# Ring loads at once, the scale's chunk first, k tiles outermost, biases ahead of the modulation

## The chip, the cores and the metric

The kernel runs on one NeuronCore of one Trainium2 chip. The metric is device time in microseconds (us) for one launch; lower is better. Five engines with their own instruction streams work side by side: TensorE (PE, its weight loads PEld), VectorE (DVE), ScalarE (ACT), GpSimd (POOL) and SyncE (SP, which here only issues DMAs). TensorE's granted clock is either 2.4 GHz (written 1.00) or 1.2 GHz (0.50).

## The reference, cut to what matters

`x` is 256 tokens by 1024 channels, float32. Five stages follow each other, each reading the `x` that the one before left:

```
h = rmsnorm(x, g) * (1 + scale) + shift        # scale, shift, gate = chunks of silu(c) @ ada_w + ada_b
x = x + gate * (mixer(h @ in_w) @ out_w)
```

The stages are called EVEN (pooling and spatial gating), ODD (gated linear attention and stick-breaking attention), F1 (SwiGLU feed-forward), MIX (short convolution and a state-space mixer) and F2 (a second SwiGLU). Between ODD and F1 stands one more rmsnorm, at the end a last one. `x` and the conditioning vectors are small; the weights, some 210 MB of float32, are read once from HBM.

## The kernel before, in words

**Number format.** Every float32 product runs as three reduced-precision (fp32r) matmuls: a weight piece is split into a high part `WH` (a copy by ACT, function `cut`, line 1083) and a low part `WL` (weight minus `WH`, by DVE, line 1505); an activation likewise into `hh`/`hl` or `YH`/`YL`. `mm3` issues high*high, high*low, low*high into one PSUM region.

**Pieces and the ring.** A unit of weights is 1 MB; it travels as two halves of 512 KB, `[128, 1024]` each, in a ring of `RING = 10` slots in SBUF. SP issues the loads in the order of `unit_list`, each waiting until the slot's last user is done. A half of a main unit is a piece: ACT cuts piece n+3 and DVE piece n+2 while PE is at piece n; `WH` and `WL` have four buffers each, freed by `s_use` when PE has used them. Between the main units stand the `ada` units (the conditioning weights), which DVE multiplies by silu(c) and sums into `ACC` (lines 1518, 1521), half by half.

**Conditioning.** A chunk is 1024 columns of `ada_w`: chunk 0 the shift, 1 the scale, 2 the gate. Each has eight halves. For the first two chunks some halves (`ADA_PE`) are done by PE instead, straight into the PSUM tensor `pacc`; for the others `ada(key)` on PE sums `ACC` over the partitions into a bank (the "sum"), and `ada(key)` on DVE adds the bias into `MOD` (the "add", line 1531) and so frees that bank. `plan` says at which unit each step stands; those with a key "tail ..." stand at a stage's end.

**Stage start.** DVE's `modulate` (lines 1595 to 1607) makes, for each of eight k tiles of 128 channels, `SQT[k] = xT[k] * GS[k] * r` (the u tile, line 1601), ACT adds the shift and rounds it to `hh[k]`, and DVE forms `hl[k]` (line 1606). PE's `cols_T`, `cols_N` and `ffn` then take a unit half by half: half 0 uses k tiles 0 to 3, half 1 uses 4 to 7, for two output tiles m; the loop over m is outside, that over k inside. One unit is 2 x 2 x 4 x 3 = 48 matmuls.

**Stage end.** `out_rows` adds two 128-row blocks (halves h = 0, 1) into the eight tiles of `pacc`. In a stage's last such unit (eo7, oo7, f1d10, wo3, f2d10) pairs of finished tiles are signalled; DVE's `update` adds them to `xT` (line 1615), ACT squares them into `SQT` (line 1118), PE sums the squares over channels (`stats`, bank `fin`), DVE takes the reciprocal root (Newton steps, lines 1564 to 1572), PE spreads it (`spread`, bank `r`). At the end of ODD PE also spreads a second factor (`xnew`, line 967). `warm` issues matmuls with no use but to keep PE busy. The four banks `pw0` to `pw3` go round by `open_` and `back`; PE waits at `open_` until a bank's last reader is done.

**Start of the program.** SP issues nine small loads (`pack_loads(0)`: c, norm_g, ada_b, ... cond), then the ring; ACT loads the identity, `x` and the rest of the constants; POOL the other small vectors. PE turns the vectors (`vc0`) and `x` (`xt0` to `xt3`) round, DVE makes `SIL` = silu(c), and the first two chunks run. The four lines of the start on DVE that matter most:

```python
cut(1 - AHEAD_L)
ada("p4")
mod_cols(0, M0, "norm_g")
modulate(L_EVEN, M0[:, 0:8])
```

Of the kernel before, what the change touches and what calls it, by code (L numbers as in the profile page):

```python
# [54 lines left out]
ADA_PE = (1, 3, 6, 11, 14)  # L55
# [45 lines left out]
def unit_list(I):  # L101
# [33 lines left out]
    units += ada(a0, 0, 2)  # L135
# [45 lines left out]
def ada_places(units, tails):  # L181
# [26 lines left out]
    at["p4"] = [("add", 0), ("add", 1)]  # L208
# [22 lines left out]
def build(nc, I, out):  # L231
    ctx = ExitStack()
    with ctx:
# [29 lines left out]
        def ar(off, n):  # L263
            return AR[:, off:off + n]
# [4 lines left out]
        def f2(ap):  # L269
# [12 lines left out]
        packs = [[("c", I["c"], 8), ("norm_g", I["norm_g"], 16), ("ada_b", I["ada_b"], 48),  # L282
                  ("pool_scale", I["pool_scale"], 8), ("sgu_norm_g", I["sgu_norm_g"], 8),
                  ("final_g", I["final_g"], 8), ("gla_gate_b", I["gla_gate_b"], 4),
                  ("gla_norm_g", I["gla_norm_g"], 8), ("cond", I["cond_2"], 8)],
# [6 lines left out]
        VR = v3(AR[:, 0:3 * P], 3)  # L292
# [47 lines left out]
        d_vec = [sem(f"d_vec{a}") for a in range(3)]  # L340
        n_vec = [16 * len(packs[0]), 16 * len(packs[1]), 16 * (len(packs[2]) + 1)]
# [78 lines left out]
        ACC2 = f2(SQT[:, 0:4, :])  # L420
# [90 lines left out]
        full, gone, place = {}, {"ada0": (s_mod, 1), "ada1": (s_mod, 2)}, {}  # L511
# [5 lines left out]
        def _(eng):  # L517
# [86 lines left out]
            def cols_N(L, name):  # L604
                k, a = unit(name)
                pb = open_(name)
                for half in range(2):
                    H, Lo = piece(2 * k + half, a)
                    for m in range(2):
                        for kk in range(4):  # L610
# [21 lines left out]
            def out_rows(L, name, i, first, last_, tail=None, mid=None):  # L632
# [3 lines left out]
                p.wait_ge(s_yl, i + 1)  # L636
                for h in range(2):
                    H, Lo = piece(2 * k + h, a)
                    for n in range(8):
                        sl = slice(n * P, n * P + P)  # L640
                        last = mm3(pacc[:, n, :], (H[:, 0, sl], Lo[:, 0, sl]), (YH[:, i % 3, h, :], YL[:, i % 3, h, :]),
                                   first and h == 0 and n % 2 == 0, last_ and h == 1)
                        if tail is not None and h == 1 and n % 2 == 1:
                            if n < 7:
                                last.then_inc(s_acc, 1)
                            else:
                                last.then_inc(s_use, 1)
                            tail(n // 2)
                    if tail is None or h == 0:
                        last.then_inc(s_use, 1)  # L650
# [32 lines left out]
            n0, n1, n2 = pack_n  # L683
# [1615 lines left out]
```

## Time and profile before

| what | us |
|---|---|
| median of 3 runs | 1064.1 (1063.83 to 1064.15) |
| the profiled execution, its own time | 1064.55 |
| span of its profile | 1062.8 |
| PE busy in it | 1011.3 |
| DVE busy | 723.7 |
| ACT busy | 508.4 |
| POOL busy | 41.6 |

The profiled execution is 1.75 us longer than its span, and 0.45 us longer than the median. A busy PE is a PE that has a matmul in flight; how fast it goes is read from the pitch of the matmuls and the granted clock.

### The profile page before, as it was taken

What the parts mean: (1) busy time and instruction counts of PE and PEld (TensorE: products, weight loads), DVE (VectorE), ACT (ScalarE), POOL (GpSimd) and SP (SyncE); (2) the same over time, 40 slices, a digit from 0 to 9 for tenths busy, and PEclk for the clock granted to TensorE, in tenths of its full rate; (3) what the DMA queues carried; (4) which work ended last, traced back from release to release, by engine and by line L of the source; (5) the groups of instructions that cost most, each with busy time, mean ns of one, the idle gap of its engine ahead of it and who ended that gap; (6) DMA issues with size and microseconds to landing.
All of it is one profiled execution on the core that took longest, in us unless ns stands there. A gap on an engine that the chain in (4) does not pass through costs nothing.

```text
span 1062.8 us, 19611 instructions
## 1 busy us (share of the span) xinstructions
PE 1011.3 (95%) x8234; PEld 998.0 (94%) x8234; DVE 723.7 (68%) x1027; ACT 508.4 (48%) x740; POOL 41.6 (4%) x69
## 2 busy tenths in 40 slices
PE   6999999999999999998899999997997999999998
PEld 5899999989999999998899999997997989999998
DVE  4767967777673855767699878668786665556454
ACT  2554354456524454634555464454546444444442
POOL 2100000000000012401000000000000000000000
PEclk9999999999999999999899999998998999999999
DMA  9976576746772876468267776755433536656631
GB/s 356 364 257 238 183 254 238 260 164 212 237 245 73 303 252 210 159 248 277 73 239 286 262 247 226 253 199 169 143 106 101 158 103 216 199 198 196 211 110 41
DMA packets 138960, 219.58 MB, mean 207 GB/s; under 512 B 7161, under 2 KB 110922, under 8 KB 138872
## 3 DMA queue, kind: packets, MB, share of 16 engines
q1 hardware_dynamic: 136776, 214.00, 58.6%
q10 hardware_dynamic: 1136, 2.58, 0.7%
q0 software_dynamic: 960, 1.76, 0.6%
q8 instruction: 65, 1.06, 0.4%
q14 instruction: 23, 0.19, 0.1%
HBM read 217.25 MB, written 1.05 MB: 205 GB/s over the span
## 4 chain that ended last, share of the span: by engine, by line
PE 86%; DVE 7%; ACT 3%; issue 2%; DMA 2%; SPq 0%; ACTq 0%; DVEq 0%
PE pw L550 64%; PE pacc L550 22%; DVE WL L1505 1%; ACT AR L1074 1%; DMA ring<-in_even_in_w 1%; DVE hl L1606 1%; DVE SQT L1601 1%; DVE ACC L1521 1%; DMA AR<-in_cond 0%; ACT WH L1074 0%; ACT hh L1074 0%; PE pw L921 0%; PE pw L709 0%; SPq L311 0%; ACT YH L1074 0%
## 5 line engine op out<-in xcount | busy, mean ns | idle before, releaser
L1074 ACT ACTIVATE WH<-ring 128x1024 fp32r<-128x1024 f32 x288 | 302.2, 1055 | 293.6 <-PE pw L550 209.3
L550 PE MATMUL pw<-hh,WH 128*128 128x256 f32 x1408 | 404.8, 288 | 14.4 <-DVE MOD L1531 6.2
L1505 DVE TENSOR_TENSOR WL<-ring,WH 128x1024 fp32r<-128x1024 f32 x288 | 344.3, 1222 | 93.7 <-ACT WH L1074 93.2
L550 PE MATMUL pw<-hl,WH 128*128 128x256 f32 x1408 | 400.5, 284 | 0.0
L550 PE MATMUL pw<-hh,WL 128*128 128x256 f32 x1408 | 400.4, 284 | 0.0
L550 PEld LDWEIGHTS pw<-hh,WH 128*128 128x128 f32 x1408 | 272.2, 193 | 19.3 <-issue 8.8
L550 PEld LDWEIGHTS pw<-hl,WH 128*128 128x128 f32 x1408 | 272.2, 193 | 0.0
L550 PEld LDWEIGHTS pw<-hh,WL 128*128 128x128 f32 x1408 | 272.1, 193 | 0.0
L550 PE MATMUL pacc<-YH,WH 128*128 128x256 f32 x672 | 191.7, 285 | 3.5 <-issue 2.5
L550 PE MATMUL pacc<-YL,WH 128*128 128x256 f32 x672 | 190.1, 283 | 0.0
L550 PE MATMUL pacc<-YH,WL 128*128 128x256 f32 x672 | 190.1, 283 | 0.0
L1074 ACT ACTIVATE AR<-pw 128x512 f32<-128x512 f32 (+6 forms) x197 | 86.7, 454 | 135.4 <-PE pw L550 134.5
L550 PEld LDWEIGHTS pacc<-YH,WH 128*128 128x128 f32 x672 | 128.9, 192 | 4.3 <-issue 4.3
L550 PEld LDWEIGHTS pacc<-YL,WH 128*128 128x128 f32 x672 | 128.9, 192 | 0.0
L550 PEld LDWEIGHTS pacc<-YH,WL 128*128 128x128 f32 x672 | 128.9, 192 | 0.0
L1521 DVE SCALAR_TENSOR_TENSOR ACC<-ring,PC,ACC 128x1024 f32<-128x1024 f32 x95 | 121.9, 1283 | 7.7 <-DMA ring<-in_ada_w 2.0
L550 PE MATMUL pw<-AR 128*128 128x64 f32 (+6 forms) x448 | 60.1, 290 | 0.9 <-ACT AR L1074 0.9
L2011 DVE TENSOR_TENSOR AR<-AR,pw 128x256 f32<-128x256 f32 x44 | 16.5, 417 | 64.0 <-ACT AR L1074 64.0
L550 PEld LDWEIGHTS pw<-AR 128*128 128x128 f32 (+3 forms) x448 | 55.1, 180 | 3.7 <-issue 1.1
L550 PE MATMUL pw<-WH,hh 128*128 128x256 f32 x192 | 55.8, 291 | 2.4 <-DVE hl L1606 2.2
L1550 DVE TENSOR_TENSOR YL<-AR,YH 128x512 fp32r<-128x512 f32 x48 | 32.8, 690 | 34.7 <-ACT YH L1074 34.6
L550 PE MATMUL pw<-WL,hh 128*128 128x256 f32 x192 | 54.9, 286 | 0.0
(245 smaller groups left out, 868.4 us busy)
## 6 DMA issues: line engine op xcount, KB each, us to landing
ring<-in_w_mod SPq DMA_DIRECT2D x72, 512.0 KB, 5.8
ring<-in_odd_in_w SPq DMA_DIRECT2D x56, 512.0 KB, 6.6
ring<-in_ada_w SPq DMA_DIRECT2D x48, 512.0 KB, 7.9
ring<-in_ffn_w_gate SPq DMA_DIRECT2D x44, 512.0 KB, 4.8
ring<-in_ffn_w_up SPq DMA_DIRECT2D x44, 512.0 KB, 5.5
ring<-in_ffn_w_down SPq DMA_DIRECT2D x44, 512.0 KB, 4.9
ring<-in_even_in_w SPq DMA_DIRECT2D x40, 512.0 KB, 6.6
ring<-in_even_out_w SPq DMA_DIRECT2D x16, 512.0 KB, 5.4
```

Source lines behind the costliest of these rows:

```text
L550: return eng.matmul(o, a, b, start=start, stop=stop, skip_group_check=True)
L1074: return eng.activation(dst, src, func, **kw)
L1505: tt(WL[:, i % NL, :], slot(half_of(i)), WH[:, i % NH, :].bitcast(F32), SUB).then_inc(s_lo, 1)
L1521: stt(out=acc, in0=slot(g), scalar=wc, in1=acc, op0=MUL, op1=ADD).then_inc(s_ada, 1)
L1550: tt(f2(YL[:, i % 3]), src, f2(YH[:, i % 3]).bitcast(F32), SUB).then_inc(s_yl, 1)
L1601: stt(out=SQT[:, k, :], in0=xT[:, k, :], scalar=GS[:, k:k + 1], in1=rb, op0=MUL, op1=MUL).then_inc(s_u, 1)
L1606: stt(out=hl[:, q, :], in0=SQT[:, q, :], scalar=m[:, q:q + 1], in1=hh[:, q, :].bitcast(F32), op0=ADD, op1=SUB).then_inc(s_hl, 1)
L2011: tt(fbuf(blk, m), fbuf(blk, m), pw[b][:, T:2 * T], MUL).then_inc(s_bank[b], 1)
```

## The change

Five things are altered.

1. **Start of the loads.** SP begins with the ring. `c` and `cond` are a pack of their own, loaded first on ACT's queue; the vectors of the former pack 0 are loaded by ACT after its two exponentials, the constants after those. POOL's `sgu` loads wait for ring half 19 instead of 15.
2. **The first two chunks.** The scale's chunk is loaded first. It is summed and added by itself; then DVE makes all eight u tiles, and goes on with the halves of the shift's chunk, whose sum and bias come in two parts of four tiles. Pieces 0 and 1 are cut between these parts. PE does six halves instead of five, DVE ten instead of eleven; `ACC2` lies in a free part of `AR`, since `SQT` now holds the u tiles.
3. **Stage ends.** The last `out_rows` unit takes both halves of a pair of tiles before the next pair. ACT cuts piece 2k+4 after the squares (`cut_on`).
4. **Biases.** At the ends of ODD and F1 DVE runs `ada("tail ...")` ahead of `modulate`, as it already does at the other ends.
5. **k tiles outermost** in `cols_T`, `cols_N` and `ffn`.

```diff
-ADA_PE = (1, 3, 6, 11, 14)
+ADA_PE = (1, 3, 6, 9, 12, 14)
...
-    units += ada(a0, 0, 2)
+    units += ada(a0, 1, 2) + ada(a0, 0, 1)
...
-    for key, ms in (("p0", (0, 2, 4)), ("p1", (5, 7, 8, 9, 10)), ("p2", (12, 13)), ("p3", (15,))):
+    for key, ms in (("p0", (0, 2)), ("p1", (4, 5, 7)), ("p2", (8,)), ("p3", (10, 11)), ("p4", (13, 15))):
...
-                    for m in range(2):
-                        for kk in range(4):
+                    for kk in range(4):
+                        for m in range(2):
...
+                if tail is not None:
+                    W = [piece(2 * k + h, a) for h in range(2)]
+                    for q in range(4):
+                        for h in range(2):
+                            for n in (2 * q, 2 * q + 1):
+                                last = product(W[h], h, n)
+                            if h == 1 and q < 3:
+                                last.then_inc(s_acc, 1)
+                            elif q == 3:
+                                last.then_inc(s_use, 1)
+                        tail(q)
+                    return
...
             squares(L_EVEN)
+            cut_on(L_EVEN)
             modulate(L_ODD, M1[:, 0:8])
...
+            ada("tail oo7")
             modulate(L_F1, M2[:, 0:8])
-            ada("tail oo7")
...
+            ada("tail f1d10")
             modulate(L_MIX, M2[:, 24:32])
-            ada("tail f1d10")
...
-            pack_loads(eng.dma_start, 0, d_vec[0])
             piece_at = {half_of(n): n for n in range(NPIECE)}
```

The first part of ACT's and DVE's programs:

```diff
+            pack_loads(eng.dma_start, 0, d_vec[0])
             eng.dma_start(cst[:, 0:P], I["consts"][:, 0:P]).then_inc(d_id, 16)
             eng.dma_start(XN, I["x"].rearrange("o (a p) n -> p (o a) n", p=P)).then_inc(d_x, 16)
-            eng.dma_start(cst[:, P:], I["consts"][:, P:]).then_inc(d_cst, 16)
...
+            pack_loads(eng.dma_start, 1, d_vec[1])
+            eng.dma_start(cst[:, P:], I["consts"][:, P:]).then_inc(d_cst, 16)
...
-            cut(1 - AHEAD_L)
-            modulate(L_EVEN, M0[:, 0:8])
+            cut(-AHEAD_H)
+            s.wait_ge(s_mod, 2)
+            modulate(L_EVEN, M0[:, 0:8], range(4))
+            cut(1 - AHEAD_H)
+            s.wait_ge(*gone["ada1"])
+            modulate(L_EVEN, M0[:, 0:8], range(4, 8))
```

**The order on DVE at the start of the program.** `MOD` is the bias add, `PC` the factor GS, `SQT` as output the u tiles (before also `ACC2`), `hl` the low parts. Before, from the last halves of chunk 0 on:

```order
L1521 SCALAR_TENSOR_TENSOR ACC<-ring,PC,ACC 128x1024 x2
L1518 TENSOR_SCALAR SQT<-ring,PC 128x1024
L1521 SCALAR_TENSOR_TENSOR SQT<-ring,PC,SQT 128x1024 x2
L1634 COPY VC<-pw 128x164
L1636 COPY AR<-AR 16x128
L1521 SCALAR_TENSOR_TENSOR SQT<-ring,PC,SQT 128x1024 x2
L1641 TENSOR_TENSOR RS<-VC,PC 128x16
L1521 SCALAR_TENSOR_TENSOR SQT<-ring,PC,SQT 128x1024
L1505 TENSOR_TENSOR WL<-ring,WH 128x1024 x2
L1526 TENSOR_TENSOR MOD<-pacc,VC 128x8 x2
L1590 SCALAR_TENSOR_TENSOR PC<-MOD,VC 128x8
L1601 SCALAR_TENSOR_TENSOR SQT<-xT,PC,pw 128x256 x2
```

Now, from the first half of the second chunk on:

```order
L1548 TENSOR_SCALAR AR<-ring,PC 128x1024
L1649 TENSOR_TENSOR MOD<-pacc,VC 128x8
L1681 SCALAR_TENSOR_TENSOR PC<-MOD,VC 128x8
L1686 SCALAR_TENSOR_TENSOR SQT<-xT,PC,pw 128x256 x8
L1551 SCALAR_TENSOR_TENSOR AR<-ring,PC,AR 128x1024 x2
L1691 TENSOR_TENSOR RS<-VC,PC 128x16
L1551 SCALAR_TENSOR_TENSOR AR<-ring,PC,AR 128x1024 x2
L1649 TENSOR_TENSOR MOD<-pacc,VC 128x4
L1535 TENSOR_TENSOR WL<-ring,WH 128x1024
L1655 SCALAR_TENSOR_TENSOR hl<-SQT,MOD,hh 128x256 x4
L1649 TENSOR_TENSOR MOD<-pacc,VC 128x4
L1535 TENSOR_TENSOR WL<-ring,WH 128x1024
```

The eight u tiles moved from behind the last half to a place four halves earlier, and piece 1 stands behind the first four low parts.

**The order on DVE at the end of ODD.** Before, the last rows of `modulate` and what follows:

```order
L1606 SCALAR_TENSOR_TENSOR hl<-SQT,MOD,hh 128x256
L1601 SCALAR_TENSOR_TENSOR SQT<-xT,PC,pw 128x256
L1606 SCALAR_TENSOR_TENSOR hl<-SQT,MOD,hh 128x256 x2
L1531 TENSOR_TENSOR MOD<-pw,VC 128x8
L1505 TENSOR_TENSOR WL<-ring,WH 128x1024
L1880 SCALAR_TENSOR_TENSOR xT<-xT,VC,pw 128x256 x2
```

Now, the last Newton steps and the first rows of `modulate`:

```order
L1594 TENSOR_TENSOR RS<-RS 128x4
L1598 SCALAR_TENSOR_TENSOR RS<-RS 128x4
L1557 TENSOR_TENSOR MOD<-pw,VC 128x8
L1627 SCALAR_TENSOR_TENSOR SQT<-xT,PC,pw 128x256 x2
L1632 SCALAR_TENSOR_TENSOR hl<-SQT,MOD,hh 128x256
```

The add that frees a bank moved from behind all sixteen instructions of `modulate` to ahead of them.

**The order on PE at the start of F1**, with the numbers of the banks. Before:

```order
L550 MATMUL pw3<-cst,RS 128x128 x2
L550 MATMUL pw0<-cst,RS 128x128 x2
L550 MATMUL pw1<-cst 128x128 x5
L550 MATMUL pw2<-hh,WH 128x256
L550 MATMUL pw2<-hl,WH 128x256
L550 MATMUL pw2<-hh,WL 128x256
L550 MATMUL pw2<-hh,WH 128x256
L550 MATMUL pw2<-hl,WH 128x256
L550 MATMUL pw2<-hh,WL 128x256
```

Now:

```order
L550 MATMUL pw2<-cst,RS 128x128 x2
L550 MATMUL pw3<-cst,RS 128x128 x2
L550 MATMUL pw0<-cst 128x128 x5
L550 MATMUL pw1<-hh,WH 128x256
L550 MATMUL pw1<-hl,WH 128x256
L550 MATMUL pw1<-hh,WL 128x256
L550 MATMUL pw0<-hh,WH 128x256
L550 MATMUL pw0<-hl,WH 128x256
L550 MATMUL pw0<-hh,WL 128x256
```

The two output tiles now take turns after three matmuls; before, one tile had twelve in a row. The second spread (`xnew`) still goes into the bank that the sum of the tail used (pw0 before, pw3 now).

## Rows read from the trace of the kernel before

**Rows 1.** The page's part 1: busy us (share of the span) xinstructions.

```profile
PE 1011.3 (95%) x8234; PEld 998.0 (94%) x8234; DVE 723.7 (68%) x1027; ACT 508.4 (48%) x740; POOL 41.6 (4%) x69
```

**Rows 2.** The chain that ended last, in order of time: start us, us, what.

```profile
21.77 10.96 DMA ring<-in_even_in_w
...
881.65 5.76 PE pacc L550 x48
887.41 11.52 PE pw L550 x96
```

**Rows 3.** Windows over the start: busy by engine, PEclk, DMA share, GB/s.

```profile
0.00:3.40 3.40, 0.00 (x0) 0.00 (x0) 0.00 (x0) 1.18 (x1) 2.26 (x8) 1.00 0.39 66
...
7.00:35.00 28.00, 24.61 (x188) 23.59 (x188) 18.19 (x33) 7.60 (x15) 3.87 (x7) 1.00 1.05 389
```

**Rows 4.** Timeline, EVEN's start: start us, us, what [idle before <-releaser].

```profile
0.81 0.39 SPq L311 DMA_DIRECT2D AR<-in_c  x1
...
4.40 15.38 SPq L2272 DMA_DIRECT2D ring<-in_ada_w  x16
...
29.74 1.28 DVE L1521 SCALAR_TENSOR_TENSOR SQT<-ring,PC,SQT 128x1024 f32<-128x1024 f32 x1 [1.29 <-DMA ring<-in_ada_w]
...
32.97 1.95 PE L550 MATMUL pw<-cst 128*128 128x128 f32 x16
...
37.14 0.36 PE L550 MATMUL pw<-WH,hh 128*128 128x256 f32 x1 [2.22 <-DVE hl L1606]
...
44.83 0.28 PE L550 MATMUL pw<-WH,hl 128*128 128x256 f32 x1
```

**Rows 5.** Windows of PE alone at two stage starts: us, PE busy (x), PEclk.

```profile
37.84:41.08 3.24, 3.24 (x14) 0.50 1.05 335
228.66:232.06 3.40, 3.40 (x16) 0.53 0.02 7
```

**Rows 6.** Timeline, ODD's start, PE and DVE.

```profile
226.39 0.36 PE L550 MATMUL pw<-hh,WH 128*128 128x256 f32 x1 [0.94 <-DVE hl L1606]
...
231.15 0.48 DVE L1606 SCALAR_TENSOR_TENSOR hl<-SQT,MOD,hh 128x256 fp32r<-128x256 f32 x1 [0.18 <-ACT hh L1074]
...
234.91 0.28 PE L550 MATMUL pw<-hh,GRH 128*16 128x256 f32 x1
```

**Rows 7.** Timeline, end of ODD and start of F1.

```profile
502.38 0.48 DVE L1606 SCALAR_TENSOR_TENSOR hl<-SQT,MOD,hh 128x256 fp32r<-128x256 f32 x1 [0.18 <-ACT hh L1074]
...
507.77 0.48 DVE L1606 SCALAR_TENSOR_TENSOR hl<-SQT,MOD,hh 128x256 fp32r<-128x256 f32 x1 [0.18 <-ACT hh L1074]
...
508.38 1.23 PE L550 MATMUL pw<-cst,RS 128*128 128x128 f32 x4 [7.10 <-DVE MOD L1531]
...
511.85 0.52 PE L550 MATMUL pw<-hh,WH 128*128 128x256 f32 x1
...
516.33 1.23 DVE L1505 TENSOR_TENSOR WL<-ring,WH 128x1024 fp32r<-128x1024 f32 x1 [3.89 <-ACT WH L1074]
...
524.22 0.75 DVE L2011 TENSOR_TENSOR AR<-AR,pw 128x256 f32<-128x256 f32 x2 [3.01 <-ACT AR L1074]
```

**Rows 8.** Windows: all engines, F1's heavy part for DVE.

```profile
536.00:556.00 20.00, 19.00 (x157) 18.49 (x155) 17.95 (x41) 11.10 (x23) 0.00 (x0) 1.00 0.58 201
```

**Rows 9.** Timeline, start of MIX.

```profile
740.27 0.48 DVE L1606 SCALAR_TENSOR_TENSOR hl<-SQT,MOD,hh 128x256 fp32r<-128x256 f32 x1 [0.18 <-ACT hh L1074]
...
740.88 0.58 PE L550 MATMUL pw<-hh,WH 128*128 128x256 f32 x1 [6.20 <-DVE MOD L1531]
...
748.43 1.22 DVE L2106 COPY AR<-pw 32x128 f32<-32x128 f32 x4 [5.26 <-PE pw L550]
```

**Rows 10.** Timeline, start of F2, PE's tenth matmul there.

```profile
859.29 0.38 PE L550 MATMUL pw<-hh,WH 128*128 128x256 f32 x1 [0.17 <-DVE hl L1606]
```

**Rows 11.** Timeline, F1's last unit: updates by DVE, PE's last sums.

```profile
725.40 2.44 DVE L1615 SCALAR_TENSOR_TENSOR xT<-pacc,PC,xT 128x256 f32<-128x256 f32 x6
...
728.10 2.84 PE L550 MATMUL pw<-cst,SQT 128*128 128x128 f32 x24
```

More of the change, by code:

```diff
@@ L509, in ysc @@
             return last
-        full, gone, place = {}, {"ada0": (s_mod, 1), "ada1": (s_mod, 2)}, {}
+        full, gone, place = {}, {"ada0": (s_mod, 1), "ada1": (s_mod, 3)}, {}
         block = ctx.enter_context(nc.Block())
@@ L636, in out_rows, with product @@
                 p.wait_ge(s_yl, i + 1)
+                def product(W, h, n):
+                    sl = slice(n * P, n * P + P)
+                    return mm3(pacc[:, n, :], (W[0][:, 0, sl], W[1][:, 0, sl]), (YH[:, i % 3, h, :], YL[:, i % 3, h, :]),
+                               first and h == 0 and n % 2 == 0, last_ and h == 1)
+                if tail is not None:
[10 more added lines that the diff above has]
+                    return
                 for h in range(2):
-                    H, Lo = piece(2 * k + h, a)
+                    W = piece(2 * k + h, a)
                     for n in range(8):
[L640 to L650, printed above, removed]
+                        last = product(W, h, n)
+                    last.then_inc(s_use, 1)
                     if mid is not None and h == 0:
@@ L713, in _ @@
             ada_half(3)
-            p.wait_ge(d_cst, 16)
-            warm(6, "warm0a")
-            spread("r0", 0, 1, (s_u, 8), True)
-            p.wait_ge(d_vec[1], n_vec[1])
-            p.wait_ge(d_vec[2], n_vec[2])
-            pb = open_("vc1")
-            eng.transpose(pb[:, 0:n1], VR[0:n1, 1, :], ident[0:n1, 0:n1])
-            close(eng.transpose(pb[:, n1:n1 + n2], VR[0:n2, 2, :], ident[0:n2, 0:n2]), "vc1")
-            ada_half(6)
-            ada_sum(0)
-            ada_half(11)
+            spread("r0", 0, 1, (s_u, 8), True)
+            pb = open_("vc1")
+            c0 = 0
+            for i, n in ((1, n1), (2, n2), (3, n3)):
+                p.wait_ge(d_vec[i], n_vec[i])
+                last = eng.transpose(pb[:, c0:c0 + n], VR[0:n, i, :], ident[0:n, 0:n])
+                c0 += n
+            close(last, "vc1")
+            ada_half(6)
+            p.wait_ge(*ada_done(7))
+            p.wait_ge(d_cst, 16)
+            ada_sum(0, range(8), "ada0")
             pb = open_("dt")
@@ L727, in _ @@
             close(eng.transpose(pb[:, 0:16], DTR, ident[0:16, 0:16]), "dt")
-            warm(8, "warm0b")
+            p.wait_ge(*gone["ada0"])
+            ada_half(9)
+            ada_half(12)
+            warm(4, "warm0a")
             ada_half(14)
-            warm(4, "warm0c")
-            ada_sum(1)
-            warm(8, "warm0d")
+            warm(4, "warm0b")
+            p.wait_ge(*ada_done(15))
+            ada_sum(1, range(4), "ada1a")
+            ada_sum(1, range(4, 8), "ada1")
+            warm(8, "warm0c")
             back("r0")
@@ L1106, in yhigh, with modulate @@
                 act(f2(YH[:, i % 3]), src).then_inc(s_yh, 1)
-            def modulate(L, sh):
-                for k in range(8):
+            def modulate(L, sh, ks=range(8)):
+                for k in ks:
                     s.wait_ge(s_u, 8 * L + k + 1)
@@ L1398, in _ @@
             squares(L_F1)
+            cut_on(L_F1)
             side.flush()
```

96 lines of the change are left out of this document (61 added, 35 removed).

## The prediction

> **What bounds the kernel now.** I read first the busy times: PE is busy for 1011.3 of 1062.8 us [rows 1], so time can only be won where PE stands still, runs at half clock or does work for nothing. Next the chain of waits, to see where it leaves PE: in mid-stage it is PE alone, at 0.12 us a matmul (11.52 / 96, and 5.76 / 48 in the other form) [rows 2]; it leaves PE at the program's start and at each of the four stage starts. Last the timeline there. Five places follow; for each I compare when PE has finished the first unit (48 matmuls) of the stage, before and now, since everything behind that repeats.
>
> **Before the first stage.** The chain goes through the ring until piece 1 lands at 32.73 (21.77 + 10.96) [rows 2]. The DMA engines moved only 66 GB/s in the first 3.4 us, then 389 GB/s up to 35 us [rows 3]: from 3.4 us on this start is bound by bytes, all of which must still come. Ring loads issued at 0.81 instead of 4.40 [rows 4] can therefore win only the bytes missing ahead of 3.4 us. If full flow begins at about 2.5 us, when the first transfers begin to show, that is 0.9 us x 389 GB/s less what moved there already: 0.7 us earlier for every later half. I take 0.7; bounds 0 and 2.
>
> The Trainium skill says in "DMA: Bandwidth & Descriptors", section "Issuing engines are not separate DMA queues", that DMAs begun by several engines run on the same 16 DMA engines and save only issue time. That speaks against a gain of the full 3.6 us by which SP begins earlier, and the 389 GB/s agrees with it; by issue time alone the start would win 2.9 us more than my 0.7.
>
> The larger part is the order behind the last half. Before, DVE takes the last half at 29.74 to 31.02; PE sums it; DVE cuts pieces 0 and 1; then bias, GS, u, hh, hl. PE, done with `warm` at 34.92, stands still for 2.22 us until the first low part, at 37.14, and the 48th matmul begins at 44.83 [rows 4]. Of these, 14 ran at half clock in 3.24 us [rows 5], about 1.6 us lost. Now: the last half lands at 29.0, but DVE has done eight u tiles in between (a u tile and a low part take (507.77 - 502.38) / 7 = 0.77 us together [rows 7], so eight u tiles about 3.1), so I let it finish at 31.4 instead of 30.3. The first half-sum takes 1.0 (eight of the 16 instructions that take `warm` 1.95), the add 0.1: 32.5. Piece 0 (1.23, as in [rows 7]) to 33.8, four low parts of 0.4 to 35.4. PE does the second half-sum and eight `warm` (1.95 us) to 35.4, so it never stands still, and keeps full clock. 48 x 0.12 = 5.8 brings it to 41.2. ACT's and DVE's piece 1 (WH after the first four hh, to 35.6; WL to 36.8) is in time for matmul 25 at 38.3, hl[7] too (38.4). Gain 44.9 - 41.2 = **3.7 us**. Bounds: 5.2 if DVE isn't behind, 0.7 if x, which now shares the engines with the ring, lands 3 us later (PE's transposes and halves queue behind it).
>
> **k tiles outermost, ODD.** PE begins at 226.39 and has the first tile's twelve matmuls paced by the low parts, 0.77 us for three; 16 at half clock [rows 5]; unit done at 234.91. hl[7] is ready at 231.63 [rows 6]. Now six matmuls (0.72 us) go with every low part, so PE keeps up and ends 0.72 behind hl[7]: 232.35, 2.6 us earlier at full clock. At half clock 16 matmuls take 3.40 and 32 take 3.84: 233.6, a gain of 1.3. I take **2.0**, since the granted clock did fall here before. Bounds 1.0 and 2.6.
>
> **F2** has the same form. There 39 matmuls remain at 859.29, so the unit ended at 864.05; now it goes by the low parts: the fourth was there at about 859.2 [rows 10], the eighth 4 x 0.77 later at 862.3, and the next piece's low part, which follows on DVE, takes 1.23: 863.5. Gain **0.6**, bounds 0 and 1.
>
> **ODD to F1.** PE waits 7.10 us for the add, which stands behind `modulate`: the second spread needs the bank that the add frees [rows 7]. The first low part was there at 502.86. After the wait come the spread, five `warm`, and only at 511.85 the first product; unit done at 511.85 + 5.8 = 517.6. With the add ahead of `modulate`, hidden by the first spread, the spreads and `warm` run under the modulation, and the products go at its pace: hl[7] at 508.25 (507.77 + 0.48) [rows 7]. What is late next is DVE: piece 2's low part follows `modulate`, 508.3 + 1.23 = 509.5, while PE would be done at 509.0. So 509.5: gain **8.1 us**. Is it kept? DVE is heavy in this stage, 17.95 of 20 us from 536 on [rows 8]. But between 508 and 524 it stood idle 3.89 and 3.01 us and some 1 us more, waiting for PE [rows 7], 8 us in all, so PE's lead is just covered. Bounds 4 and 8.5.
>
> **F1 to MIX.** PE waits 6.20 us for the same add, then runs 14 matmuls at half clock; unit done shortly ahead of 748.43, where DVE, idle for 5.26 us, takes it over [rows 9]. Now hl[7] at 740.75, piece 2 at 740.8 + 1.23 = 742.0. At 748.2 before, 742.0 now: gain **6.2 us**, and 5.26 of DVE's idle time cover it. Bounds 4 and 6.8.
>
> **Stage ends.** The tile pairs come sooner, but what ends last there is PE's own sums, 2.84 us for three pairs behind the last product (24 instructions at 728.10) [rows 11]; neither DVE nor ACT is waited for, so nothing is won. There is a loss where the updates are late: in F1 DVE begins them at 725.40, whatever order PE has, and PE can't sum the first pair until about 1 us later; behind that sum stand now 12 products instead of 6: +0.7 us. In ODD, where DVE is less late, I take +0.2. Sum **-0.9**, bounds -2 and +0.5. ACT's piece moved behind the squares lies under the Newton steps and costs nothing; POOL's loads, later by about 5 us, are needed only after four units of PE work.
>
> **Sum.** 3.7 + 2.0 + 8.1 + 6.2 + 0.6 - 0.9 = 19.7 us. From the profiled execution's own 1064.55 (span 1062.8) that gives 1044.85; it lies 0.45 above the median, and from the median, 1064.1, it is 1044.4.
>
> **The rivals.**
> *DVE takes over (1051.5).* PE begins F1 and MIX while DVE is still modulating, with no lead of DVE's over PE. If the 8 and 5 us of DVE's idle time are spread so that they can't be used, half of 8.1 + 6.2 comes back as waits for WL in 509 to 560 and 742 to 800: 7.1 us. For it: the 17.95 of 20 us [rows 8]. Against: the idle times are long and lie right there.
> *The start stays bound by bytes (1047.4).* Only 0.7 us of the 3.7 is won, if x comes late or DVE is behind by all u tiles. For it: 389 GB/s up to 35 us [rows 3]. Against: the 2.22 us of idle PE and the half clock lie behind the last byte.
> *The wait stays (about 1057).* If another reader held the bank, PE would wait at F1 and MIX as before and the change would not do what it says; 3.7 + 2.0 + 0.6 - 0.9 and 2 for the k order remain. The only add moved is the one named as releaser, so this is unlikely.
> *Slower (from 1064 on).* Two accumulators taking turns after three matmuls could cost PE at each switch. There are 1600 such triples (3 x 1408 + 3 x 192 matmuls); 19.7 us are gone at 12.3 ns each, and at 25 ns the time is 1084. Against: `out_rows` already changes its accumulator after three matmuls and runs at the same 0.12 us [rows 2]. The Trainium skill tells in "TensorE: Matmul & The Clock Gate", section "A second HAM failure mode: psum-queue depth-cycling", of a kernel that went round PSUM banks and lost its full clock between bursts; by that rule `ffn`, now on two banks in turn, would be slow. No row here shows it.
>
> **How the numbers follow.** Forecast 1044.4, chance 0.62, own range 1041 to 1048; DVE takes over 0.18; the start bound by bytes 0.12; the wait stays 0.03; slower 0.03; no difference 0.02. The range must hold 8 in 10: low 1039.5 (the upper bounds of start, ODD and F2), high 1053 (the first two rivals, and part of both). A measurement of this kernel tells 0.2% (2.1 us) from no change: faster 0.95, same 0.02, slower 0.03.
>
> **What would show it.** PE's first product with `hh` at about 35.4, its 48th done near 41.2, granted clock 1.00 there. No wait for MOD at the starts of F1 and MIX; PE's first products there within 0.5 us of the first low part, paced by `hl`, and one short wait for WL. DVE's idle time behind these starts gone. A wait of about 1 us for ACT's squares at F1's end. Wrong would be: a fallen clock at a stage start, waits for WL of over 3 us in F1, a pitch other than 0.12 us in mid-stage, or PE's transposes of x later than 10 us.

## The result, and the profile after

The changed kernel takes 1046.12 us (median of 4 runs, 1045.77 to 1048.05), the kernel before 1064.12 beside it: ratio 0.9835, 95% interval 0.9818 to 0.9852, so 18.0 us or 1.65% faster. The forecast was 1044.4, range 1039.5 to 1053. The profiled execution took 1046.0 with a span of 1044.3 us, 18.5 less than the 1062.8 of before.

The page's part 1 of the changed kernel, to be held against [rows 1]:

```profile
PE 1003.0 (96%) x8231; PEld 990.5 (95%) x8231; DVE 722.1 (69%) x1027; ACT 506.7 (49%) x740; POOL 41.7 (4%) x69
```

PE has the same work and is busy for 8.3 us less. Part of that is less time at half clock: the mean granted clock of the profiled execution rose from 0.983 to 0.995. The other 10 us are time in which PE no longer stands still.

To see where the time went I cut the span at pieces of the chain that every version has: the transposes of `sgu_w` in EVEN, the last 24 sums of a stage, the first products into `pacc` of F1 and F2, and so on. The chain of the changed kernel at these marks (start us, us, what):

```profile
60.64 0.87 PE pw L757 x8
...
217.37 2.69 PE pw L550 x24
...
256.32 20.42 PE pw L550 x168
...
491.61 6.27 PE pw L550 x56
...
544.43 5.99 PE pacc L550 x48
...
717.26 2.70 PE pw L550 x24
...
796.99 6.01 PE pw L550 x36
...
808.62 1.79 PE pw L550 x16
...
831.87 2.69 PE pw L550 x24
...
863.06 5.76 PE pacc L550 x48
```

The table gives the time between neighbouring marks in the profiled execution of each kernel (differences of such start times; `e1` and so on are the experiments below; `e8` is the changed kernel once more, `e12` the kernel before with filler matmuls in four waits). It is the tool for all that follows: a cause that sits in one place changes one line.

| from mark to mark | before | e12 | e1 | e2 | after | e8 | e3 | e4 | e5 | e9 |
|---|---|---|---|---|---|---|---|---|---|---|
| A start to EVEN's transposes | 62.39 | 62.08 | 62.58 | 61.78 | 60.64 | 61.08 | 61.74 | 58.32 | 58.47 | 58.44 |
| B to EVEN's last sums | 156.67 | 155.51 | 156.75 | 155.47 | 156.73 | 155.45 | 155.45 | 155.46 | 155.45 | 155.53 |
| C over ODD's start | 41.28 | 39.94 | 41.30 | 39.97 | 38.95 | 38.94 | 38.96 | 38.96 | 38.93 | 38.96 |
| D to ODD's last sums | 234.69 | 236.21 | 234.70 | 235.28 | 235.29 | 234.96 | 234.69 | 236.50 | 234.77 | 234.70 |
| E over F1's start | 61.12 | 61.35 | 53.51 | 53.50 | 52.82 | 52.81 | 52.82 | 52.83 | 52.80 | 52.83 |
| F to F1's last sums | 172.11 | 170.63 | 170.65 | 171.36 | 172.83 | 172.85 | 172.12 | 172.85 | 170.63 | 170.63 |
| G over MIX's start | 85.76 | 86.56 | 80.28 | 80.25 | 79.73 | 79.71 | 79.73 | 79.72 | 79.70 | 79.71 |
| H MIX, around `glu` | 12.50 | 10.07 | 12.64 | 13.96 | 11.63 | 14.13 | 11.57 | 14.10 | 11.61 | 10.08 |
| I to MIX's last sums | 23.25 | 23.25 | 23.63 | 23.25 | 23.25 | 23.25 | 23.26 | 23.25 | 23.25 | 23.25 |
| J over F2's start | 31.88 | 31.89 | 31.90 | 33.19 | 31.19 | 31.20 | 31.19 | 31.20 | 31.20 | 31.19 |
| K to the end | 181.15 | 181.21 | 181.16 | 181.19 | 181.24 | 181.22 | 181.17 | 181.21 | 181.19 | 181.18 |
| span | 1062.8 | 1058.7 | 1049.1 | 1049.2 | 1044.3 | 1045.6 | 1042.7 | 1044.4 | 1038.0 | 1036.5 |

Two things are seen at once. K, 181 us of mid-stage F2, is the same in all of them: matmuls that take turns between two accumulators run at the old pace. And B, C, D, F, H and J also take values that do not follow the edits, mostly in steps of 1.2 to 1.5 us (B is 155.5 or 156.7; `after` and `e8` are the same kernel and differ in B by 1.28 and in H by 2.50). That is the granted clock, below. Line A varies too: with the changed start and x issued as in the change it is 60.64 (after), 61.08 (e8), 61.74 (e3) and 61.78 (e2). The profile of `after` is the shortest of the four.

**The start, changed kernel.** Timeline of PE and DVE (start us, us, what, [idle before <- releaser]):

```profile
12.69 3.46 PE L718 MATMUL pw<-cst,AR 128*128 128x128 f32 x16 [5.55 <-DMA AR<-in_x]
...
14.89 0.17 DVE L1580 TENSOR_SCALAR RS<-RS 128x2 f32<-128x2 f32 x1 [4.23 <-ACT AR L1089]
...
33.46 2.05 PE L550 MATMUL pacc<-cst,AR 128*128 128x128 f32 x16 [1.41 <-DVE AR L1551]
35.35 1.95 PE L550 MATMUL pw<-cst 128*128 128x128 f32 x16
37.06 0.36 PE L550 MATMUL pw<-WH,hh 128*128 128x256 f32 x1
```

PE goes from `warm` to the first product without a gap, at full clock (1.00 over 35.51 to 43.04); the 2.22 us and the half clock of [rows 4, 5] are gone. But x lands at 12.65, PE waits 5.55 us and DVE 4.23 us for it, and from then on DVE is late: PE waits for it again at 33.46, and the first product is at 37.06 where 35.4 was forecast.

**The start of F1.** The same view, with DVE's piece 2 and its next idle time:

```profile
499.58 0.35 PE L550 MATMUL pw<-hh,WH 128*128 128x256 f32 x1 [0.16 <-DVE hl L1632]
...
504.75 1.22 DVE L1535 TENSOR_TENSOR WL<-ring,WH 128x1024 fp32r<-128x1024 f32 x1
...
513.01 0.36 PE L550 MATMUL pw<-hh,WH 128*128 128x256 f32 x1 [0.97 <-issue]
```

No row waits for MOD any more. PE's first product follows the first low part after 0.16 us, is paced by `hl`, and the piece of low parts that comes behind the modulation is cut at 504.75, as forecast. DVE's idle times of [rows 7] (3.89 and 3.01) are gone: between 504 and 545 its waits are 0.18, 0.76, 0.67 and 0.76, 2.4 us in all.

### The profile page after: what moved, and what is told of

The parts are those of the page before. It is cut to its first block, busy times and chain, and to the rows that moved or that the text cites. A ratio compares the mean times of both kernels' runs of the same rounds, so it can differ in the third digit from the quotient of the medians.

```text
span 1044.3 us, 19611 instructions
## 1 busy us (share of the span) xinstructions
PE 1003.0 (96%) x8231; PEld 990.5 (95%) x8231; DVE 722.1 (69%) x1027; ACT 506.7 (49%) x740; POOL 41.7 (4%) x69
## 4 chain that ended last, share of the span: by engine, by line
PE 85%; DVE 8%; ACT 3%; issue 2%; DMA 1%; ACTq 0%; DVEq 0%
PE pw L550 63%; PE pacc L550 22%; DVE WL L1535 2%; ACT AR L1089 1%; DMA AR<-in_x 1%; DVE hl L1632 1%; DVE SQT L1627 1%; DVE ACC L1551 1%; DVE AR L1551 0%; ACT WH L1089 0%; ACT hh L1089 0%; PE pw L936 0%; PE pw L718 0%; DVE SQT L1686 0%; ACT YH L1089 0%
## 5 line engine op out<-in xcount | busy, mean ns | idle before, releaser
L550 PE MATMUL pw<-WH,hl 128*128 128x256 f32 x192 | 54.3, 283 | 0.0
```

The lines of the kernel that those rows point to most:

```text
L550: return eng.matmul(o, a, b, start=start, stop=stop, skip_group_check=True)
```

## The experiments

The runs e1 to e4 were made on one occasion, e5 to e8 on a second, e9 to e12 on a third and on another chip. `after` was measured apart from e1 to e4, and again as e8 (1047.09 against 1046.12), so a difference of 1 us between medians of different occasions says little; the lines of the table say more.

**e1: only the two bias additions ahead of `modulate`.**

```diff
--- before
-            modulate(L_F1, M2[:, 0:8])
             ada("tail oo7")
+            modulate(L_F1, M2[:, 0:8])
...
-            modulate(L_MIX, M2[:, 24:32])
             ada("tail f1d10")
+            modulate(L_MIX, M2[:, 24:32])
```

> The kernel before with one thing of the change: DVE adds the scale-and-shift bias (the two tail adds) ahead of modulate at the ends of ODD and F1. Nothing at the start, no k order, no regrouped last unit. Theory (the add was the releaser, and the lead is kept): F1 gains 8.1 less about 0.5 for the old k order, MIX 6.2 less about 0.5, no loss at the stage ends: 13.3 us in all, about 1050.8; PE's wait for MOD is gone at both places and shows as short waits for hl. Rival (DVE takes over): half comes back in F1 and MIX, about 1057, with waits for WL or the gate's products in mid-stage. Rival (another reader holds the bank): within 2 us of 1064.

Measured: 1050.88 (1048.51 to 1051.04), before 1064.37; 13.5 us gained. Line E of the table gains 7.61, G 5.48, together 13.09; the rest of the span's 13.7 is mostly F, 1.46 less, where the clock did not fall this time. PE's waits at F1's start:

```profile
503.32 0.35 PE L550 MATMUL pw<-hh,WH 128*128 128x256 f32 x1 [0.17 <-DVE hl L1606]
...
505.59 0.39 PE L550 MATMUL pw<-hh,WH 128*128 128x256 f32 x1 [0.17 <-DVE hl L1606]
```

So the add was the releaser and the whole of the 7.10 us of [rows 7] can be had; both rivals fall. Two lines that change places carry 13.1 of the 18.5 us.

**e2: the changed kernel with the column tile m outermost again** (in `cols_T`, `cols_N` and `ffn`).

```diff
--- after
-                    for kk in range(4):
-                        for m in range(2):
+                    for m in range(2):
+                        for kk in range(4):
```

> The changed kernel with the three loops turned back: column tile m outside, k tile inside. Theory (k order lets PE keep up with the low parts at the stage starts): ODD's start is 2.3 us later, with the granted clock at half for some matmuls there, F2's 0.7 later, and F1's, MIX's and EVEN's about 0.5 each: 4.5 us slower than the changed kernel, about 1050.6. Rival (alternating accumulators cost PE something in mid-stage): mid-stage is faster than 0.12 us a matmul and the time is within 2 us of the changed kernel or below it.

Measured: 1049.94 (1049.1 to 1050.93), 3.8 slower than the changed kernel. ODD (C) is 1.02 later, F1 (E) 0.68, MIX (G) 0.52. The clock did not fall in ODD this time, so 1.02 is the k order alone and the other 1.31 of C's 2.33 is the half clock of [rows 5]. That fall is not fixed either: in e12, whose code at ODD's start is that of the kernel before, it is absent (C is 39.94). With m outermost it came in two profiles of four, with k outermost in none of ten (e3 to e11 and `after`). That the k order prevents it is likely, but not shown. In e2 the clock fell in F2 instead (J is 2.00 longer; e1, with m outermost and no fall there, shows 0.71 for the order itself). Windows of PE alone over F2's start, e2 first, then the changed kernel (us, PE busy (x), PEclk, DMA share, GB/s):

```profile
842.00:850.00 8.00, 7.52 (x44) 0.79 0.04 6
```

```profile
842.00:850.00 8.00, 7.89 (x64) 1.00 0.38 110
```

With k outermost PE has six matmuls for each low part and hardly waits. The rival, a cost of alternating accumulators, would have to show in K: 181.19 against 181.24. At EVEN's start, where 0.5 us was expected, the k order is worth nothing: from the start of the pieces that lead to the first product (36.66 in e2, 35.51 in `after`) to the end of line A it is 25.12 and 25.13 us. That A is 1.14 longer in e2 arises before, at x's transposes and the first halves.

**e3: the changed kernel with the old order in the last unit** (first all eight tiles of piece 0, then the pairs of piece 1).

```diff
--- after
-                if tail is not None:
-                    W = [piece(2 * k + h, a) for h in range(2)]
-                    for q in range(4):
-                        for h in range(2):
-                            for n in (2 * q, 2 * q + 1):
-                                last = product(W[h], h, n)
...
+                        if tail is not None and h == 1 and n % 2 == 1:
...
+                            tail(n // 2)
```

> The changed kernel with the old order in the last unit of each stage's out product: all eight tiles of piece 0, then the tile pairs of piece 1 with their sums between them. ACT's and DVE's cutting order as in the changed kernel. Theory (regrouping puts six more products behind a late first pair at F1's end and at ODD's, and wins nothing elsewhere): 0.7 to 0.9 us faster than the changed kernel, about 1045.3. Rival (the pairs coming sooner win something at the stage ends): 0.5 to 2 us slower, 1046.6 to 1048.

Measured: 1044.16 (1043.75 to 1045.13), 2.0 faster than the changed kernel where 0.7 to 0.9 was expected. By the table D gains 0.60 and F 0.71; lines B (EVEN) and I (MIX) don't differ beside the clock's step. The rest does not come from the edit: B is free of the fall (-1.28), and A is 1.10 longer, PE taking 7.98 instead of 7.03 us for x's transposes and the first halves behind its long wait for x. Why it takes longer there stays open; the granted clock is 1.00 in both. At ODD's end, chain of e3, then timeline of the changed kernel:

```profile
455.35 33.88 PE pacc L550 x282
489.22 0.89 PE pw L550 x8
490.12 0.72 PE pacc L550 x6
```

```profile
489.01 1.16 PE L550 MATMUL pw<-RS,SQT 128*128 128x128 f32 x8 [0.33 <-ACT SQT L1089]
...
491.44 2.84 PE L550 MATMUL pw<-RS,SQT 128*128 128x128 f32 x24
```

The old order has six products more ahead of the first sum, so PE never waits; the new one waits 0.33 for the square and its eight sums, paced by the squares, take 1.16 instead of 0.89: 0.60 in all. In e8, the same kernel, the wait of 0.33 is absent, and D is only 0.27 longer than in e3. So ODD's price is 0.3 to 0.6. The regrouping loses at two stage ends and wins at none.

**e4: x issued by SP ahead of the ring**, instead of by ACT behind the small loads.

```diff
--- after
             eng.dma_start(cst[:, 0:P], I["consts"][:, 0:P]).then_inc(d_id, 16)
-            eng.dma_start(XN, I["x"].rearrange("o (a p) n -> p (o a) n", p=P)).then_inc(d_x, 16)
...
             y = Eng(eng, None)
+            eng.dma_start(XN, I["x"].rearrange("o (a p) n -> p (o a) n", p=P)).then_inc(d_x, 16)
             piece_at = {half_of(n): n for n in range(NPIECE)}
```

> The changed kernel with the load of x issued by SP ahead of the ring, instead of by ACT behind c, cond and the identity. Theory (x comes late because it shares the DMA engines with ring loads issued before it; PE's transposes and DVE's halves queue behind it): x lands near 7 instead of 12.65 us, DVE has taken the last half by about 31.5 instead of 33.4, and the ring lands 1 to 1.3 us later (its own issue time and the bytes of x ahead of it), so 1 to 2 us are won: about 1044.5. Rival (bytes alone bound the start: the last half lands at the same time whatever is ahead): within 0.5 us of the changed kernel, with DVE idle before the last half. Rival (the ring's delay costs more than x's lead gains): 1 us slower, about 1047.

Measured: 1044.01 (1043.29 to 1046.12), 2.1 faster. Line A: 58.32 against 60.64 (61.08 to 61.78 in the other three profiles with the late x), and 4.07 less than before. Timeline of the start:

```profile
8.46 3.67 PE L718 MATMUL pw<-cst,AR 128*128 128x128 f32 x16
...
14.00 0.17 DVE L1579 TENSOR_SCALAR RS<-RS 128x2 f32<-128x2 f32 x1 [1.95 <-ACT AR L1089]
...
31.14 2.05 PE L550 MATMUL pacc<-cst,AR 128*128 128x128 f32 x16 [0.24 <-DVE AR L1550]
33.03 1.95 PE L550 MATMUL pw<-cst 128*128 128x128 f32 x16
34.74 0.36 PE L550 MATMUL pw<-WH,hh 128*128 128x256 f32 x1
```

From the list of DMA issues, x in the changed kernel and in e4 (engine, count, KB, us from issue to landing):

```profile
AR<-in_x ACTq DMA_DIRECT2D x1, 1024.0 KB, 10.5
```

```profile
AR<-in_x SPq DMA_DIRECT2D x1, 1024.0 KB, 4.9
```

PE transposes x at 8.46 instead of 12.69, DVE has taken the last half at 31.1 (31.4 in the prediction) and the first product is at 34.74 (35.4). The late x was the cause; the bytes were not. e7 shows the same by another edit.

**e7: the changed order of work, but nine small loads on SP ahead of the ring**, as before the change. ACT then issues the identity and x first.

```diff
--- after (ACT)
-            pack_loads(eng.dma_start, 0, d_vec[0])
...
-            pack_loads(eng.dma_start, 1, d_vec[1])
--- after (SP)
             y = Eng(eng, None)
+            pack_loads(eng.dma_start, 0, d_vec[0])
+            pack_loads(eng.dma_start, 1, d_vec[1])
```

> The changed kernel with the nine small constant loads of the first two packs issued by SP ahead of the ring, as before the change, instead of by ACT. ACT begins with the identity and x, so x is ahead of the ring again; the ring's first load is issued near 4.4 instead of 0.8 us. The order of work behind stays as changed. Theory (x late costs 2 to 3 us, the ring late costs 0.7): x lands near 7 us and 1.5 to 2.5 us are won against the changed kernel, 1044.5, and about 0.7 to 1 are lost against x alone ahead. Rival (bytes bound the start, so 3.6 us of later issue cost most of 3.6): 1 to 3 us slower than the changed kernel, 1047 to 1049.

Measured: 1044.02 (1042.32 to 1046.7), with the unaltered changed kernel (e8) at 1047.09 beside it, so 3.1 faster although the ring begins at 4.11 instead of 0.8 us. The ranges of the two overlap; line A, 2.1 us shorter than in e8, does not. Line A is 58.97: 0.65 more than with x ahead and the ring at once (58.32). In e4 the ring begins at 1.28, so 2.8 us of earlier issue are worth about 0.65 (line A of the kernels with x ahead, e4, e5, e6, e9 and e11, lies between 58.23 and 58.51, so 0.5 to 0.7); 0.7 had been put down for it.

```profile
6.97 3.67 PE L718 MATMUL pw<-cst,AR 128*128 128x128 f32 x16 [3.73 <-DMA AR<-in_x]
```

x, issued by ACT, lands at 6.97 when no ring load is ahead of it, and at 12.65 when they are (changed kernel). Of these 5.7 us, 0.9 are its later issue (2.15 against 1.23); from issue to landing it is 10.5 against 5.7.

**e8 and e5: the changed kernel once more, and both mends together** (the edits of e3 and e4).

> The changed kernel unaltered, as the mark for the three runs beside it on the same chip. By what went before: a median near 1046.1. If the granted clock falls by chance behind PE's short waits in mid-stage (in EVEN near 139 us, in MIX near 795 to 806), its runs lie in steps between 1043.5 and 1048; if the falls are fixed for a kernel, all lie within 0.3 us.

> The changed kernel with both mends: x issued by SP ahead of the ring, and the old order in the last unit of each stage. Theory (two separate places, so the gains add): 2.3 to 3.4 us at the start (seen with x ahead alone) and 0.6 + 0.7 at the ends of ODD and F1 (seen with the old order alone), so 3.6 to 4.7 us faster than the changed kernel: 1041.4 to 1042.5. Rival (what is won at the start is lost behind it to weights that come later): 1044.

Measured: e8 1047.09 (1045.46 to 1047.87); e5 1040.53 (1039.57 to 1041.48), ratio to before 0.9777 (0.9762 to 0.9793). The expected 3.6 to 4.7 became 6.6 between the medians. In the table e5 has A 58.47, D 234.77, F 170.63: against `after` the gains add (2.2 + 0.5 + 0.7), and B and F are free of the falls of the clock that the profile of `after` has (1.3 and 1.5). Against e8 beside it, A gives 2.6 and D 0.2, F 0.7 by the edit and 1.5 by the clock, and H 2.5 by the clock. So the edits are worth 3.4 to 3.5 us, a little below what was expected, and the rest is fewer falls in this run. The four runs of e8 lie 2.4 us apart, as the first of the two forecasts for it says.

**e6 and e9: fillers in four waits of PE**, on top of both mends.

```diff
--- both mends
+            def heat(n, pb, start=True):
+                for _ in range(n):
+                    mm(pb[:, 384:512], ident, ones, start)
...
-                        p.wait_ge(s_yl, g + 1)
                         pb = open_(f"pool{g}")
+                        if g == 2:
+                            heat(6, pb)
+                        p.wait_ge(s_yl, g + 1)
...
                     pb = open_("cs")
+                    heat(6, pb)
                     for n in range(4):
+                        if n == 2:
+                            heat(4, pb, False)
...
+                if name == "wo0":
+                    heat(9, f2(pacc[:, 0:2, :]))
                 p.wait_ge(s_yl, i + 1)
```

> The kernel with both mends, and matmuls for nothing put into four waits of PE in mid-stage: 6 (f32, 128 x 128, about 0.24 us each) ahead of the third pool group in EVEN, where PE waits 1.77 us; 6 and 4 ahead of and within the conv statistics of MIX, where it waits 1.93 and 1.36; 9 ahead of MIX's out product, where it waits 2.51. They fill waits only, and change no result. Theory (the clock falls by chance because PE stood still there): granted clock 1.00 in EVEN 136 to 150 and in MIX 790 to 812, 1 to 2.5 us faster than the kernel with both mends alone: 1040 to 1041, and its runs lie closer together. Rival (the waits have nothing to do with the clock, or the fillers delay the work that PE waits for): the same or up to 1 us slower, with half clock still shown there.

> The kernel with both mends and the fillers in PE's four waits, as in the run before it, but with the four fillers inside the conv statistics adding to unused columns instead of starting a group anew, since a new start in the bank lost the sums already there. The same number of instructions at the same places. Expected: the same time as that run, 1038.1 to 1038.5, within 0.3 us, with granted clock 1.00 in EVEN 136 to 150 and MIX 790 to 812, and 2 us faster than the kernel with both mends alone.

(e6 gives a wrong result, since it lost sums of the conv statistics by starting a group anew; its work is else that of e9.) Measured: e6 1038.3 (1038.11 to 1039.55), 2.2 faster than e5 beside it. e9 1039.78 (1038.24 to 1041.24), ratio to before 0.9764 (0.975 to 0.9777); it was measured on another chip than e5, and its runs are spread over 3 us, not the 0.3 that was expected. Its best run equals e6. The intervals of its ratio and of e5's overlap, so the gain of the fillers in the whole time rests on e6 against e5; their effect at their places is in line H. Windows of PE alone over 790 to 812 in the changed kernel, in the same kernel once more (e8), in e5 and in e9:

```profile
790.00:812.00 22.00, 16.21 (x121) 0.92 0.39 121
```

```profile
790.00:812.00 22.00, 16.23 (x100) 0.77 0.38 116
```

```profile
790.00:812.00 22.00, 18.74 (x144) 0.92 0.35 105
```

```profile
790.00:812.00 22.00, 21.03 (x177) 1.00 0.38 108
```

In e9 the clock is 1.00, and line H is 10.08 where it was 11.6 to 14.1. The mean granted clock of e9's profiled execution is 1.000; in its three slower runs it is 0.997 to 0.998.

**e12: the kernel before, with the same fillers and nothing else.**

> The kernel before, with nothing of the change, but with the fillers in the four waits of PE (third pool group, conv statistics twice, ahead of MIX's out product). Theory (the falls of the clock behind these waits are apart from the change): EVEN 136 to 150 and MIX 812 to 820 at full clock, 1.2 to 1.3 us won in EVEN and 0.9 to 2.5 in MIX: 1060.5 to 1062. Rival (in the kernel before the clock falls at other places instead): within 0.5 us of before.

Measured: 1060.63 (1060.09 to 1061.12), ratio 0.996 (0.9946 to 0.9973): 3.8 us. Line H is 10.07, as in e9, and B 155.51. So the time that the fillers win has nothing to do with the change. Elsewhere it is chance as before: in this execution C and F are free of a fall (1.3 and 1.5 less), and D has one (236.21, 1.5 more, clock 0.96 between 450 and 490, where no filler stands). G is 0.8 longer: the 472 matmuls from MIX's start on take 57.83 us instead of 57.04.

**e10: u tiles behind the last four ring halves** (DVE), on e9.

```diff
--- e9
-            for k in range(8):
-                stt(out=SQT[:, k, :], in0=xT[:, k, :], scalar=GS[:, k:k + 1], in1=pw[place["r0"]][:, 0:T],
-                    op0=MUL, op1=MUL).then_inc(s_u, 1)
...
             ada("p4")
+            for k in range(8):
+                stt(out=SQT[:, k, :], in0=xT[:, k, :], scalar=GS[:, k:k + 1], in1=pw[place["r0"]][:, 0:T],
+                    op0=MUL, op1=MUL).then_inc(s_u, 1)
             first_add(1, 0, 0, 4, "ada1a")
```

> The kernel with both mends and the fillers, with DVE's eight u tiles moved back behind the last four ring halves, ahead of the second bias. Theory (the u tiles fill time in which DVE would wait for the ring): DVE takes the last half 1 to 2 us earlier, at 29 to 30, limited by its landing, but has the 3.2 us of u tiles still before it, so PE's first product is 1.2 to 2.2 us later and the time about 1039.5 to 1040.5. Rival (DVE is behind anyway with x ahead, so the order doesn't matter): within 0.4 us of the kernel beside it.

Measured: 1041.26 (1039.81 to 1043.1) against e9's 1039.78: 1.5 slower. The ranges overlap; line A, 59.92, is 1.48 more. Timeline of DVE and PE:

```profile
26.82 1.28 DVE L1556 SCALAR_TENSOR_TENSOR AR<-ring,PC,AR 128x1024 f32<-128x1024 f32 x1 [1.62 <-DMA ring<-in_ada_w]
29.61 1.28 DVE L1556 SCALAR_TENSOR_TENSOR AR<-ring,PC,AR 128x1024 f32<-128x1024 f32 x1 [1.51 <-DMA ring<-in_ada_w]
...
35.77 0.36 PE L550 MATMUL pw<-WH,hh 128*128 128x256 f32 x1 [0.99 <-DVE hl L1660]
```

Here DVE waits 3.1 us for the ring, which is what the u tiles (3.2 us) fill otherwise. The last half lands at about 29.6 (29.0 in the prediction).

**e11: 4.2 us of useless work on DVE at F1's start**, on e9.

```diff
--- e9
             modulate(L_F1, M2[:, 0:8])
+            for _ in range(12):
+                v.wait_ge(*v.step(stt(out=DUM[:, :], in0=xT[:, 0, 0:96], scalar=M2[:, 0:1], in1=xT[:, 1, 0:96],
+                                      op0=MUL, op1=ADD)))
```

> The kernel with both mends and the fillers, with 12 dependent instructions of no use on DVE (128 x 96, about 0.2 to 0.25 us each, 2.4 to 3 us in all) behind the modulation at F1's start. In the changed kernel DVE stood idle for 2.4 us between 504 and 545, where it was 10.3 between 508 and 556 before. Theory (DVE's idle time there is used up by the early start of PE, so that DVE now sets F1's first 40 us): 2.0 to 3.0 us slower, near 1041, as waits of PE for WL in 510 to 545. Rival (DVE is still well ahead of PE, and the gain of the early add doesn't hang on its idle time): less than 1 us slower.

Measured: 1044.66 (1043.92 to 1048.31), 4.9 slower than e9. The 12 took 4.21 us, more than the 2.4 to 3 they were meant to; line E is 59.07 instead of 52.83, 6.24 more.

```profile
501.10 4.21 DVE L1936 SCALAR_TENSOR_TENSOR DUM<-xT,MOD 128x96 f32<-128x96 f32 x12
...
506.63 0.58 PE L551 MATMUL pw<-hh,WH 128*128 128x256 f32 x1 [4.35 <-DVE WL L1541]
...
515.11 0.75 DVE L2075 TENSOR_TENSOR AR<-AR,pw 128x256 f32<-128x256 f32 x2 [2.00 <-ACT AR L1096]
```

Windows of PE alone behind that wait:

```profile
506.63:512.00 5.37, 5.37 (x28) 0.57 0.60 195
```

All of the added time is paid, and about 2 us more because the clock fell behind a wait of 4.35 us. But it is paid at the first unit already: the low parts of piece 2 stand directly behind the added work, and DVE idles again afterwards (2.00). So DVE has no slack at the moment of the start; that it is short over the whole of 504 to 545 is not shown by this run. The theory as I wrote it (waits spread over 510 to 545) was wrong in its place, right in sign.

## Why the prediction held, term by term

| term | forecast | measured | where it is read |
|---|---|---|---|
| start | 3.7 | 1.75 | A |
| ODD's start | 2.0 | 2.33 | C |
| ODD to F1 | 8.1 | 8.30 | E |
| F1 to MIX | 6.2 | 6.03 | G |
| F2's start | 0.6 | 0.69 | J |
| stage ends | -0.9 | -0.60 - 0.72 | D, F |
| not forecast: clock in MIX | 0 | +0.87 | H |
| B, I and K | 0 | -0.15 | B, I, K |
| sum | 19.7 | 18.5 | span |

**Start.** The order of work was right, and with x ahead e4 gives 4.07 for the start. The step that failed is the assumption in the sum that x comes as early as before. It stood among the bounds ("0.7 if x, which now shares the engines with the ring, lands 3 us later") and was not taken, and by the prediction's own sign of being wrong, "PE's transposes of x later than 10 us", the start did not go as forecast: they began at 12.69. The late x cost 2.3 us between the profiles of `after` and e4, and up to 3.5 by the other profiles of the changed start, where the gain of line A is only 0.6 to 1.3. What it delays is seen in the chain: PE's transposes of x and the halves behind them, and with them DVE's u tiles, begun at 25.23 in `after` and at 22.90 in e4:

```profile
25.23 2.82 DVE SQT L1686 x7
```

```profile
22.90 2.83 DVE SQT L1685 x7
```

The rival "the start stays bound by bytes" had a late x among its conditions, and that condition came true. Its title is not what the runs show: e4 and e7 move the same bytes and are faster. That the ring's early begin is worth 0.7 agrees with e7's 0.65. PE's sixth half and the later loads of POOL were not tested apart.

The Trainium skill says in "DMA: Bandwidth & Descriptors", "Issuing engines are not separate DMA queues", that DMAs of different engines run on the same 16 DMA engines and interleave, and that starting them on several engines saves only the issue time. The trace agrees that they share: x took 10.5 us from issue to landing beside the ring's loads, and 5.7 in e7 ahead of them. Even the issue time was not saved in full: 2.8 us of it were worth 0.65.

**ODD, F2.** 2.0 was taken between 1.0 and 2.6; it became 2.33 because the clock stayed at 1.00 this time. e2 splits it: 1.02 from the k order, 1.31 from the clock. The fall in the profile of the kernel before was partly luck of the comparison, since e2 and e12 avoid it with m outermost: against e12 the gain in C would be 0.99.

**F1 and MIX.** 8.30 and 6.03 against 8.1 and 6.2. e1 puts 7.61 + 5.48 on the two moved additions; the rest, 0.68 + 0.52, is the k order (e2), which lets PE finish with the last low part. "DVE takes over" did not come: DVE's idle time between F1's start and 40 us on fell from 10.3 to 2.4 us, the 8 us that the prediction counted. PE's wait of 0.97 there is no new one: it stands in the kernel before too, at 523.77.

**Stage ends.** F1 as forecast (0.71 in e3, forecast 0.7); ODD cost 0.60 in this profile and 0.27 in e8's, where 0.2 was forecast. There too the squares come late for a PE that has only twelve products ahead of its first sum; I had put this down for F1 alone. PE's wait for ACT's square at F1's end, forecast at about 1 us, is 0.87.

**Slower by alternating accumulators.** K says no: 181.24 against 181.15 over the most even stretch. The granted clock is 1.00 from 863 to 1021, in F2's `ffn`, which now goes round two banks. The Trainium skill tells in "TensorE: Matmul & The Clock Gate", "A second HAM failure mode: psum-queue depth-cycling", of a kernel that cycled through banks and stood still for moments between its groups of matmuls, and ties the falls of the clock to these idle moments. The prediction had left that condition out. PE is busy for 157.2 of these 158 us, so the trace does not speak against the section; it shows that turns between two banks alone don't bring the fall.

**The clock, which the prediction had only at two stage starts.** H, which it did not name, gave 0.87 of the gain by chance; without it the profiled gain is 17.6. In e8 the same line is 1.63 longer than before instead. With the 1.31 of ODD's start, some 2 us of the profiled 18.5 hang on where the clock fell in these two executions. That the profiled gain comes within 1.2 us of the forecast is in part luck: the start won 1.9 us less than forecast, and H's 0.9 and ODD's 0.3, both of the clock, made up for some of it.

**The range.** The low end, 1039.5, is said to be the upper bounds of start, ODD and F2. With the other terms as forecast these three give 22.2 us, so 1041.9; 1039.5 needs the upper bounds of all six terms (24.6). The measured time lies inside either way.

The two mends make a kernel of 1040.53, and with the fillers of 1039.78. Against the kernel before, run beside each (1064.03 and 1064.47), that is 23.5 and 24.7 us, of which 18 are the change's.

## What to carry to other kernels

Look for an addition that frees a buffer and stands behind work that doesn't need it: moving the two here gave 13 of 18 us, and the wait that named it was in the timeline. When a queue is moved to the front, ask what it overtakes: the first thing that several engines need (here x) must be issued ahead of the bulk, even if the bulk begins 3 us later. And before a difference of one or two us is put down to an edit, cut both traces at marks that all versions share; what stands in a line that the edit doesn't touch is most likely not the edit's.

## What the runs showed of the hardware

**The granted clock falls behind short waits of PE, in some executions and not in others.** Line B is 156.7 or 155.5 with the same instructions. PE stands still for 1.77 us in it in all kernels without fillers (at 139.17 in `after`, 140.91 before). Windows of PE alone, 136 to 150, of the changed kernel and of the same kernel once more, e8 (us, PE busy (x), PEclk, DMA share, GB/s):

```profile
136.00:150.00 14.00, 12.23 (x90) 0.88 0.83 298
```

```profile
136.00:150.00 14.00, 12.20 (x100) 1.00 0.86 301
```

In MIX three waits of 1.93, 1.36 and 2.51 us follow one another, and every profile without fillers has half clock behind them, at a price of 1.5 to 4.0 us in line H. The timeline of the changed kernel there; from one matmul to the next it is 0.22 us first, then 0.12:

```profile
794.50 1.13 PE L550 MATMUL pw<-cst,SQT 128*128 128x128 f32 x8 [1.93 <-ACT SQT L1089]
...
799.11 0.41 PE L550 MATMUL pw<-YH,WH 128*128 128x256 f32 x1
799.33 0.41 PE L550 MATMUL pw<-YL,WH 128*128 128x256 f32 x1
...
801.33 0.28 PE L550 MATMUL pw<-YH,WH 128*128 128x256 f32 x1
801.45 0.28 PE L550 MATMUL pw<-YL,WH 128*128 128x256 f32 x1
```

These are the two levels, 1.2 and 2.4 GHz. It is the likely cause of the 2 to 3 us between runs of one kernel: of the four runs of `after` the longest (1048.05) has the lowest mean granted clock (0.993) and the shortest (1045.77) the highest (0.996), and it is the same in e9 (1041.24 at 0.997, 1038.24 at 1.000). The profiles of `after` and e8, 1.3 us apart, differ by it in B and H. Filled waits removed it at their own places (H 10.07 and 10.08 with fillers, 11.6 to 14.1 without), not at others. What decides whether it falls behind a given wait of 1 to 2.5 us stays open; two executions with the same instructions differ.
